# A conv module's first stage: gate weights in three blocks, the first product ahead of the parameter transposes, channel sums on VectorE

## What is computed

```
def conv_module(x, past, w_pw1, b_pw1, w_dw, b_dw, g_cn, b_cn, w_pw2, b_pw2):
    h = x @ w_pw1 + b_pw1                                  # D -> 2D, D = 1024
    u = h[..., :D_MODEL] * jax.nn.sigmoid(h[..., D_MODEL:])
    ext = jnp.concatenate([past.astype(u.dtype), u], axis=1)
    conv = depthwise_conv(ext, w_dw, width 31, causal) + b_dw
    z = layer_norm(conv, g_cn, b_cn)                       # over the 1024 channels
    z = z * jax.nn.sigmoid(z)
    return z @ w_pw2 + b_pw2, ext[:, -CONV_STATE:]
```

## Time and profile before

| | |
|---|---|
| median of 3 runs | 1152.04 us |
| runs | 1146.96 to 1158.1 us |
| profiled execution | 1158.06 us |
| its span, first to last instruction | 1156.4 us |
| TensorE, VectorE, ScalarE busy | 85%, 29%, 15% of the span |
| mean granted TensorE clock | 0.915 of full |

### The profile page before, as it was taken

How to read it: one execution, slowest core, us unless ns; L and a number is a source line. 1 busy time by engine, 2 the same in 40 slices (tenths; PEclk the granted TensorE clock), 3 DMA queues, 4 the chain that set the end, 5 groups by cost and what they waited for, 6 DMA issues and landing times.

```text
span 1156.4 us, 14202 instructions
## 1 busy us (share of the span) xinstructions
PE 987.6 (85%) x4754; PEld 490.2 (42%) x4755; DVE 336.6 (29%) x792; ACT 168.1 (15%) x327; POOL 104.3 (9%) x196
## 2 busy tenths in 40 slices
PE   3989978899889989859989775479798999988994
PEld 2656535443334333336556443244443333333331
DVE  2555454422112211141234331211531112212115
ACT  1000032111011100111123221111111011101001
POOL 2050000101000000032000011200020000000000
PEclk9999988799999999979889897789888999999897
DMA  8485444999779999956030111219565579999981
GB/s 213 124 275 144 134 173 164 332 376 341 283 276 374 374 377 386 355 167 219 14 146 1 41 46 51 86 40 393 203 201 193 208 268 374 381 377 373 384 329 46
DMA packets 131605, 267.18 MB, mean 231 GB/s; under 512 B 7370, under 2 KB 39142, under 8 KB 131539
## 3 DMA queue, kind: packets, MB, share of 16 engines
q1 hardware_dynamic: 121184, 237.75, 58.3%
q0 software_dynamic: 5392, 12.60, 4.2%
q10 hardware_dynamic: 4979, 16.15, 3.8%
HBM read 260.04 MB, written 7.15 MB: 231 GB/s over the span
## 4 chain that ended last, share of the span: by engine, by line
PE 70%; DMA 11%; DVE 9%; SPq 4%; ACT 3%; issue 3%; ACTq 0%; DVEq 0%; POOL 0%
PE bank L948 19%; PE bank L956 10%; DMA w<-in_e_w 6%; PE wide L991 5%; PE bank L881 4%; PE bank L769 3%; PE bank L935 3%; PE wide L881 2%; PE wide L769 2%; PE bank L1682 2%; DMA w<-in_state_conv 2%; PE bank L785 2%; PE bank L1583 2%; DMA dbuf<-in_a_w_pw 2%; PE bank L1562 2%
## 5 line engine op out<-in xcount | busy, mean ns | idle before, releaser
L948 PE MATMUL bank<-w,dbuf 128*64 128x512 f32 x1024 | 236.8, 616 | 15.1 <-DMA w<-in_e_w 12.1
L948 PEld LDWEIGHTS bank<-w,dbuf 128*64 128x64 f32 x1024 | 80.0, 142 | 165.2 <-issue 163.2
L956 PE MATMUL bank<-w,dbuf 128*64 128x512 f32 x512 | 131.6, 661 | 11.0 <-DVE dbuf L1361 10.3
L1366 DVE COPY dbuf<-bank 64x512 f32<-64x512 f32 x64 | 44.1, 688 | 166.3 <-PE bank L956 165.9
L1357 DVE TENSOR_TENSOR dbuf<-dbuf,bank 64x512 f32<-64x512 f32 x32 | 22.1, 690 | 208.5 <-ACT dbuf L696 208.5
L696 ACT ACTIVATE dbuf<-bank 64x512 f32<-64x512 f32 x32 | 18.9, 591 | 421.5 <-PE bank L948 421.5
L956 PEld LDWEIGHTS bank<-w,dbuf 128*64 128x64 f32 x512 | 43.1, 150 | 82.5 <-issue 82.3
L991 PE MATMUL wide<-dbuf,ukT 128*128 128x512 f32 (+1 forms) x144 | 70.3, 615 | 6.0 <-DVE dbuf L1382 3.0
L1682 PE MATMUL bank<-ident,w 128*128 128x128 f32 (+1 forms) x192 | 34.4, 335 | 36.3 <-DMA w<-in_cache_ckv 28.6
L935 PEld LDWEIGHTS bank<-ident,dbuf 64*128 64x128 f32 x476 | 41.3, 160 | 51.7 <-issue 41.7
L935 PE MATMUL bank<-ident,dbuf 64*128 64x64 f32 x476 | 50.6, 244 | 10.6 <-DVE dbuf L1366 3.4
(11 more groups left out here) (343 smaller groups left out, 1102.2 us busy)
## 6 DMA issues: line engine op xcount, KB each, us to landing
w<-in_e_w SPq DMA_DIRECT2D x90, 2048.0 KB, 20.0
dbuf<-in_a_w_pw SPq DMA_DIRECT2D x16, 512.0 KB, 6.2
w<-in_cache_ckv SPq DMA_DIRECT2D x64, 128.0 KB, 2.4
w<-u_rows SPq DMA_DIRECT2D x32, 142.0 KB, 2.9
dbuf<-in_a_w_pw ACTq DMA_DIRECT2D x1, 4096.0 KB, 16.7
dbuf<-in_e_w SPq DMA_DIRECT2D x2, 2048.0 KB
dbuf<-in_b_w_o SPq DMA_DIRECT2D x1, 4096.0 KB, 12.9
x_tok<-in_e_w SPq DMA_DIRECT2D x2, 1536.0 KB
```

Of the source, the lines that this page charges most:

```text
L948: last = nc.tensor.matmul(bank[n * C:(n + 1) * C], x[:, k], w[n][k], start=(k == 0), stop=(k == KD - 1))
L956: last = nc.tensor.matmul(bank[n * C:(n + 1) * C], h[:, k], w[k][:, n * 512:(n + 1) * 512], start=(k == 0), stop=(k == 3))
L1366: last = V.tensor_copy(y_pair[s * C:(s + 1) * C, h * 512:(h + 1) * 512], DOWN[h * C:(h + 1) * C, :])
```

## The change

The gate weights come in three blocks instead of eight: channels 0 and 1 in two loads of 1 MB, which are waited for before SyncE issues anything else, then four channels in two loads of 2 MB into `w13[0]`, then two in two loads of 1 MB into `w2[0]`. (Both buffers are expert 0's; its loads now wait for the last gate product.) TensorE does `gated(0)` right behind xT, ahead of the parameter and state transposes, and its second half waits for a semaphore of its own. GpSimd's loads wait for that first product, ScalarE issues the state's loads behind the xT copies, and VectorE does `glu(0)` before the tap columns. The channel sums of blocks 0 to 6 are added by VectorE (`sum_channels`, `sum_squares`) into `sum_c` and `sum_sq`, and TensorE sums these two and block 7 with four matmuls at the end.

```diff
-        pw1 = [part(dbuf, s * 2048, KD, 2, P) for s in range(2)]
+        pw1 = [part(dbuf, 0, KD, 2, 2 * P), part(w13[0], 0, KD, 2, 4 * P), part(w2[0], 0, KD, 2, 2 * P)]
+        PW1_BLOCKS = [(0, 2), (2, 4), (6, 2)]
...
+        sum_c, sum_sq = part(dbuf, 13312, T), part(dbuf, 13632, T)
...
-            for s in range(2):
-                load_pw1(s, s)
-            sp.wait_ge(glu_done, 2)
+            for q, (j0, n) in enumerate(PW1_BLOCKS):
+                if q == 1:
+                    sp.wait_ge(pw1_ready[0], 16)
+                    sp.wait_ge(pw1_ready[1], 16)
+                for h in range(2):
+                    sp.dma_start(pw1[q][:, :, h], w1v[:, :, h, j0 * P:(j0 + n) * P])\
+                        .then_inc(pw1_ready[h if q == 0 else q + 1], 16)
+            sp.wait_ge(glu_done, 3)
             for j in range(KD):
-                if j + 2 < KD:
-                    sp.wait_ge(h_done, j + 1)
-                    load_pw1(j + 2, j % 2)
                 replicate(j)
...
+            sp.wait_ge(h_done, KD)
             load_13(0, 0, 0)
...
+            pool.wait_ge(h_done, 1)
             pool.dma_start(rw[:], a["r_w"].rearrange("(k p) e -> p k e", p=P)).then_inc(ld_misc, 16)
...
+            act.wait_ge(ones_set, 1)
+            nc.scalar.activation(spare2[:, 1:2], spare2[:, 0:1], ACT.Sigmoid)
+            copy_xT(act, 0)
             for h in range(2):
                 act.dma_start(state[0:4 * CS, h],
                               a["state_conv"][0, 4 * h:4 * h + 4].rearrange("b s d -> (b s) d")).then_inc(ld_state, 16)
-            act.wait_ge(ones_set, 1)
-            nc.scalar.activation(spare2[:, 1:2], spare2[:, 0:1], ACT.Sigmoid)
-            copy_xT(act, 0)
...
-                act.wait_ge(glu_done, j + 1)
+                act.wait_ge(glu_done, max(1, j + (j > 2)))
...
+            def add_channels():
+
+                pe.wait_ge(chan_summed, 2)
+                nc.tensor.matmul(B[4][:, 0:T], ones[:], sum_c, start=True, stop=False)
+                nc.tensor.matmul(B[5][:, 0:T], ones[:], sum_sq, start=True, stop=False)
+                pe.wait_ge(acc_done, 2 * KD)
+                nc.tensor.matmul(B[4][:, 0:T], ones[:], acc[:, KD - 1], start=False, stop=True).then_inc(sum_done, 1)
+                pe.wait_ge(sq_done, KD)
+                nc.tensor.matmul(B[5][:, 0:T], ones[:], sq[(KD - 1) % 2], start=False, stop=True).then_inc(sq_used, 1)
+
+            pe.wait_ge(xT_copied, 6)
+            gated(0)
             pe.wait_ge(ld_vec, 16 * (len(VECS) + 1))
             nc.tensor.transpose(B[2][:, 0:NVEC], vec_rows[0:NVEC], ident[0:NVEC, 0:NVEC])
...
+            def sum_channels(j):
+
+                dve.wait_ge(acc_done, 2 * j + 2)
+                if j == 0:
+                    mark(V.tensor_copy(sum_c, acc[:, 0]))
+                else:
+                    dve.wait_ge(dve_seq, seq[0])
+                    ins = V.tensor_tensor(sum_c, sum_c, acc[:, j], ALU.add)
...
+            def sum_squares(j):
+
+                dve.wait_ge(sq_done, j + 1)
+                if j == 0:
+                    V.tensor_copy(sum_sq, sq[0]).then_inc(sq_summed, 1)
+                else:
+                    dve.wait_ge(sq_summed, j)
+                    ins = V.tensor_tensor(sum_sq, sum_sq, sq[j % 2], ALU.add)
...
             for j in range(KD):
-                glu(j)
+                if j:
+                    glu(j)
+                if j >= 5:
+                    sum_squares(j - 5)
                 samples(j)
...
                     finish_block(j - 2)
                     set_taps(j)
+                    sum_channels(j - 2)
+            sum_squares(3)
             finish_block(KD - 2)
+            sum_channels(KD - 2)
+            for j in range(4, KD - 1):
+                sum_squares(j)
             finish_block(KD - 1)
```

More of the change, by code:

```diff
@@ L194, in trunk_step @@
         tap_w = [part(ukT_buf, s * 1024, GROUPS, STEPS, 32) for s in range(2)]
-        tap_col = part(dbuf, 13904, KD, GROUPS, STEPS)
+        tap_col = part(dbuf, 13952, KD, GROUPS, STEPS)
         pick32 = sb("pick32", [P, 32])
@@ L294, in trunk_step @@
         ld_x = [sem(f"ld_x{i}") for i in range(3)]
-        pw1_ready = [sem("pw1_ready0"), sem("pw1_ready1")]
+        pw1_ready = [sem(f"pw1_ready{i}") for i in range(4)]
         pw2_ready, ln_ready = sem("pw2_ready"), sem("ln_ready")
@@ L308, in trunk_step @@
         mix_done = sem("mix_done")
+        chan_summed, sq_summed = sem("chan_summed"), sem("sq_summed")
         u_packed = sem("u_packed")
@@ L375, in sp_program @@
             w1v = a["a_w_pw1"][0].rearrange("(k p) (h c) -> p k h c", p=P, h=2)
-            def load_pw1(j, s):
-                for h in range(2):
-                    sp.dma_start(pw1[s][:, :, h], w1v[:, :, h, bass.ts(j, P)]).then_inc(pw1_ready[s], 16)
             def replicate(j):
@@ L741, in pe_program, with gated @@
                 turn_tile(pe, 0, 0, i)
+            def gated(j):
+                s = j % 2
+                q = 0 if j < 2 else 1 if j < 6 else 2
+                at = (j - PW1_BLOCKS[q][0]) * P
+                if j == 1:
+                    pe.wait_ge(glu_done, 1)
+                elif j:
+                    pe.wait_ge(pw1_ready[q + 1], 32)
+                    pe.wait_ge(glu_done, max(2, j + (j > 2)))
+                    pe.wait_ge(glu_p, j - 1)
+                for h in range(2):
+                    if j == 0:
+                        pe.wait_ge(pw1_ready[h], 16)
+                    for k in range(KD):
+                        last = nc.tensor.matmul(B[2 * s + h][:, 0:T], pw1[q][:, k, h, at:at + P], xT[:, k], start=(k == 0),
+                                                stop=(k == KD - 1))
+                last.then_inc(h_done, 1)
@@ new lines, in conv @@
+            def conv(j):
+                pe.wait_ge(tap_w_set, j + 1)
+                pe.wait_ge(copied[j % 2], (j // 2 + 1) * 16 * SHIFTS)
+                if j >= 2:
+                    pe.wait_ge(first_done, 1)
+                    if j >= 3:
+                        pe.wait_ge(acc_done, 2 * j - 2)
+                else:
+                    pe.wait_ge(glu_done, 3)
+                for q in range(STEPS):
+                    for g in range(GROUPS):
+                        last = nc.tensor.matmul(B[6 + j % 2][32 * g:32 * g + 32, 0:SEQ], tap_w[j % 2][:, g, q],
+                                                copies[j % 2][:, g, 4 * q:4 * q + SEQ], start=(q == 0),
+                                                stop=(q == STEPS - 1))
+                last.then_inc(conv_done, 1)
@@ new lines, in pivot @@
+            def pivot():
+                pe.wait_ge(first_done, 2)
+                nc.tensor.matmul(B[5][:, 0:T], ones[:], acc[:, 0], start=True, stop=True).then_inc(pivot_done, 1)
+            def add_channels():
[6 more added lines that the diff above has]
+                nc.tensor.matmul(B[5][:, 0:T], ones[:], sq[(KD - 1) % 2], start=False, stop=True).then_inc(sq_used, 1)
@@ L1083, in dve_program, with glu @@
                 .then_inc(glu_done, 1)
+            def glu(j):
+                s = j % 2
+                dve.wait_ge(sig_done, j + 1)
+                V.scalar_tensor_tensor(ext[:, j, CS:EXTP], B[2 * s][:, 0:SEQ], vec_T[:, j:j + 1], sig[s][:, 0:SEQ],
+                                       ALU.add, ALU.mult).then_inc(glu_p, 1)
+                V.scalar_tensor_tensor(ext_s[:, j, :, CS:EXTS],
+                                       B[2 * s][:, SEQ:T].rearrange("p (b s) -> p b s", b=DB), vec_T[:, j:j + 1],
+                                       sig[s][:, SEQ:T].rearrange("p (b s) -> p b s", b=DB),
+                                       ALU.add, ALU.mult).then_inc(glu_done, 1)
+            dve.wait_ge(pad_set, 1)
+            glu(0)
             dve.wait_ge(ld_ident, 16)
@@ L1158, in finish_block @@
                                        ALU.subtract).then_inc(acc_done, 1)
+            def sum_channels(j):
[5 more added lines that the diff above has]
+                    ins = V.tensor_tensor(sum_c, sum_c, acc[:, j], ALU.add)
+                    if j < KD - 2:
+                        mark(ins)
+                    else:
+                        ins.then_inc(chan_summed, 1)
+            def sum_squares(j):
+                dve.wait_ge(sq_done, j + 1)
+                if j == 0:
+                    V.tensor_copy(sum_sq, sq[0]).then_inc(sq_summed, 1)
+                else:
+                    dve.wait_ge(sq_summed, j)
+                    ins = V.tensor_tensor(sum_sq, sum_sq, sq[j % 2], ALU.add)
+                    if j < KD - 2:
+                        ins.then_inc(sq_summed, 1)
+                    else:
+                        ins.then_inc(chan_summed, 1)
             set_taps(0)
```

63 lines of the change are left out of this document (4 added, 59 removed).

## The result

The changed kernel took 1143.51 us (median of ten runs, 1134.82 to 1149.65) beside 1151.99 for the kernel before (ten runs, 1146.40 to 1158.10): ratio 0.9923, 95% interval 0.9896 to 0.9951, that is 8.5 us (by the medians) or 0.8% faster. The forecast of 1128.0 us was wrong, and the time lies outside its range. A gain is there, but a third of the one forecast.

The account below looks back on a forecast made before the run. Bound taken: the first stage's TensorE chain, idle early for loads and before the fifth gate product. Terms put the mean at 121.3 against 145.27, 24.0 us earlier: 1134.1 profiled, 1128.0 on the median's basis; range 1120 to 1140.

Parts of the forecast that it names:

- (a): Start of gate product 0: block 0's first half lands and the product starts at 10.7 us, bounds 7.3 and 21.9.
- Rival 3: Block 0 still lands as late as 21.9 us; product 2 ends at 52.8, 8.3 lost, 1136.3 us; chance 0.07.
- (b): Length of gate product 0: starts cold and takes 10.28 us, ending at 21.0.
- (c) and (d): Parameter transposes 1.3 us, then state transposes 2.1 us behind product 0, ending at 24.4, with the state landed in time.
- rival 2: State lands late, at 32.7; product 2 ends at 54.9, 10.4 us lost, 1138.4 (milder case 1131.3); chance 0.08.
- (f): Start of conv 0: waits for block 0's copies until 44.5 us, against 41.7 without a wait; bounds 41.7 and 50.5.
- (e): Gate products 1 and 2: 8.63 us each, ending at 41.7, with block 1 down near 30.
- rival 1: Conv 0's bounce is held up further by 6.3 MB in its queue: conv 0 at 50.5, 1134 us; chance 0.12.
- (g): Conv 0 to the end of product 7: 62.2 us instead of 71.8, without idle, slow clock and 4.1 of sums.
- (h): Tail from product 7 to the mean: 14.6 us instead of 17.04; conv 7 bound by the last copies at 9.3.
- (i): VectorE's 14 added sum operations, 6.9 us in all, cost zero; up to 2 us without the tail's cover.
- Rival 4: Slower: the bounce bounds three blocks if stores take 19.6 us, 1157.7 us; decides from 17.7 mean landing; chance 0.03.

Follow-up runs that it names:

- the version with all three late: Changed kernel with taps loaded as 16 and 15 rows, block 2 behind the second bounce, pw2 at block 4, GpSimd's loads behind the fourth gate product: 1128.43 us, ratio 0.9814.
- the control: The version with all three late, but with GpSimd's loads back behind the first gate product: 1130.74 us, one run.
- the late version with the taps whole: The version with all three late, but with the 31 tap rows back in one transfer: 1139.03 us, one run.

## Why the prediction was wrong, step by step

The mean was forecast at 121.3 and came at 136.46, 15.2 us later. The steps:

- **(a), start of product 0: 10.7 forecast, 21.41 measured, +10.7.** This is the step that failed, and the largest term. The sum took the bytes ahead over a rate of all 16 engines, 317 GB/s. For 15 of them that was about right: at 14 us nearly all of both halves was there (13.8 forecast). The landing is that of the slowest engine, and 124 KB of taps and then state rows stood on it. Rival 3 named the outcome ("block 0 still lands as late as 21.9") with a chance of 0.07; the argument against it, that q0 and the state are out of the way, looked at the queues' totals where the earlier trace rows already showed one loaded engine after 20 us. It put the end of product 2 at 52.8 (52.08 measured), but let conv 0 follow without a wait, so its price of 8.3 us was too small as well. The split decides the start: 12.69 with it, 21.41 without. That 12.69 is still 2.0 later than 10.7 goes with a lower rate: in the run with the taps split the engines moved 212 and 242 GB/s from 6 to 8 and 8 to 10 us, not 317.
- **(b), 10.28 forecast, 10.84 measured; (c) and (d), 3.4 forecast, 2.6 measured.** The first product is 0.6 longer. That it started cold can be read from its lengths only: some 8 of its 32 matmuls run in its first 4.0 us, the others in 6.8, while the row gives a granted clock of 1.00 for both; in the version with all three late the row gives 0.50 for the first 3.2 us of product 0. The transposes behind it ran at a granted clock of 1.00, and the state was down in time (landed 9.3 us after its issue at the latest, by 20.7 us): rival 2 did not happen, though its rule on the one engine did, to another load. (The milder price of rival 2, 1131.3, adds 3.3 us to the forecast that belong to the floor of (f), 41.7; from 45.0 instead of 44.5 it would be 1128.5.)
- **(e), 17.2 forecast and measured.** In the changed kernel it held only because product 0 was late. "Block 1 is down near 30" was wrong: with product 0 at 12.69 block 1 landed at 35.82, and product 2 waited. GpSimd's loads, which the change issues at the end of product 0, are part of that (4.3 us in the control).
- **(f), conv 0 at 44.5 forecast, 56.21 measured.** Of the 11.7 us, 10.4 are (a) to (d), and 1.3 is a longer wait (4.13 instead of 2.8). In the changed kernel the store was issued at 42.95 (31.6 forecast, so 11.4 later) and landed in 7.7 us, and its copies in 2.4 to 4.1; pw2 was issued only at 52.1, behind them. The small number hides a large error: with product 0 in time the wait is 10.26 and conv 0 comes at 55.01. In that run the store had been priced about right (9.4 forecast, 9.8 measured), its copies not: 3.0 us had been taken from the earlier trace rows, and beside pw2 they took up to 9.2. The price of rival 1, conv 0 at 50.5, was too small. So (f) is a second step that failed, hidden behind (a): two limits in a row stood at 55 to 56 us. With the first taken away the mean came at 133.95 (time 1136.63), with the second (the late version with the taps whole) at 131.53 (1139.03, one run): either alone is 10 to 13 us behind the forecast mean, though both times lie inside the range; the changed kernel, with both, lies outside.
- **(g), 62.2 forecast from conv 0 to the end of product 7, 65.8 measured (56.21 to 121.98).** Conv 0 itself took 5.29 instead of 3.66, cold after its wait, and conv 1 waited 1.44 us for copies: 3.1 of the 3.6.
- **(h), 14.6 forecast, 14.5 measured**, and conv 7 started 9.0 us after product 7 (9.3 forecast), bound by the copies as forecast. Here a reader must be careful; this is the timeline of that place, of the kernel after:

```profile
125.67 2.47 SPq L390 DMA_DIRECT2D w<-u_rows  x4
...
128.53 1.22 DVE L1115 TENSOR_TENSOR ukT<-pick,dbuf 128x1024 f32<-128x1024 f32 x1
...
130.47 0.48 DVE L1157 SCALAR_TENSOR_TENSOR w<-bank,vec_T,dbuf 128x256 f32<-128x256 f32 x1
...
130.95 3.66 PE L778 MATMUL bank<-w,ukT 128*32 128x256 f32 x64 [1.94 <-DVE w L1157]
```

The bracket names VectorE's finish of block 6 (L1157). But conv 7 waits for acc_done 12, which block 5 has given already at 128.6, and its taps were there at 129.75. The last copy was issued at 127.0 and landed up to 3.9 us later, at 130.9. The releaser is inferred from what ended last before the start, and there two things ended together. The version with all three late, whose conv 7 has the same waits, settles it: there conv 7 starts 0.2 us before the finish of block 6 ends (114.09 + 0.48), and the bracket names the copies.

```profile
114.35 3.66 PE L783 MATMUL bank<-w,ukT 128*32 128x256 f32 x64 [1.72 <-DMA w<-u_rows]
```

- **(i), the sums on VectorE cost nothing: right**, and the 4.1 + 2.4 = 6.5 us that (g) and (h) credit to them was measured as 6.6. VectorE's last sum ended at 133.26, before conv 7 did (134.61).
- **Rival 4**, slower, did not happen: no store took longer to land than 11.4 us where it needed 17.7.

What is measured and what is inferred: the taps on one engine, block 2 ahead of the store, pw2 beside the copies and GpSimd beside block 1 have each been taken away or put back alone. Why the copies suffer from pw2, whose rows are four times as long as theirs, was not tried. The scatter of the time behind the stage was not tried.

## What to carry to other kernels

A transfer lands when its slowest engine is done: before dividing bytes by a rate, ask over how many engines each small transfer ahead of it is spread, on every queue. A load of 31 rows split as 16 and 15 was worth 9 us where nothing else bound. When a load is made to come sooner, put everything that is not needed yet (later weights in the same queue, bulk loads on others) behind the small round trips that now decide, and price a round trip by its landing in that company, not in a quiet stretch. Hold a change of several parts against each part alone: here the part worth 6 us hid that the others, as made, were worth little, and that together with the split taps and the three issues moved they were worth some 18.

## What the runs showed of the hardware that was not expected

- 124 KB in 31 rows on ScalarE's queue, with the state behind it, held up to 118 KB of a 2 MB load on SP's queue back by some 8 us, though the rest of it was there. The Trainium skill, "DMA: Bandwidth & Descriptors", section "Why a DMA increments its semaphore by 16 and not by 1", gives the count of engines by the slowest dimension (31 rows: one engine, 16 rows: sixteen, 15 rows: fifteen); the runs agree with it as far as they show it (a share of 5.8% where one engine of 16 is 6.25%; 20.4 us to landing whole, 12.8 split), and add what it does to others.
- The issue of a DMA can hold its queue's engine for long: the four issues of blocks 1 and 2 took 12.45 us on SP's queue in the run with the taps split, and the store behind them 3.12 us instead of 0.34.
- A small round trip has no price of its own: copies that land in 2.5 to 3.1 us alone took up to 9.2 beside pw2 in the run with the taps split, and up to 11.5 (those of block 1) in the changed kernel. The store of block 0 took 9.8 us with block 2 ahead of it and GpSimd's loads beside it, 5.3 with the loads alone, 1.8 with neither.
- The clock after a short idle time isn't the same from run to run. Before conv 7 TensorE was idle for 1.94 us in one kernel and 1.98 in another; in the run with the taps split it was idle for 2.17 and the conv took 3.66 at a granted clock of 1.00. This is the window of conv 7 in the kernel with the 1.98, the late version with the taps whole (columns as in the earlier trace rows):

```profile
124.30:129.60 5.30, 5.27 (x64) 3.30 (x64) 2.07 (x5) 0.64 (x2) 0.00 (x0) 0.68 0.99 369
```

Its granted clock is 0.68, part of it at the 1.2 GHz level, and the conv took 5.35 us; in the changed kernel the same conv took 3.66 at a granted clock of 1.00. In a sum, the end of a stage has such a term of 1.7 us that may or may not come; what decides it, the runs don't show.
